# Statistics with one token a partition for three RMS norms, and another order of values, residuals, squares and weight splits at their joins

## What is computed

```python
def rmsnorm(x, g):
    xf = x.astype(jnp.float32)
    y = xf * lax.rsqrt(jnp.mean(xf * xf, axis=-1, keepdims=True) + EPS)
    return (y * g.astype(jnp.float32)).astype(x.dtype)
...
h = rmsnorm(x, norm_g[layer, 0]) * (1 + sc1) + sh1
y = mixer(h)                        # layer 0: convolution and retention; layer 1: attention
x = x + g1 * y
h = rmsnorm(x, norm_g[layer, 1]) * (1 + sc2) + sh2
x = x + g2 * (jnp.square(jax.nn.relu(h @ mlp_w1[layer])) @ mlp_w2[layer])
```

## Time and profile before

| | us |
|---|---|
| median of 3 runs | 1574.41 |
| lowest, highest | 1573.16, 1574.59 |
| the profiled execution | 1574.52 |
| its span in the profile | 1572.7 |
| TensorE busy | 1552.5 |
| VectorE busy | 985.1 |
| ScalarE busy | 625.1 |
| GpSimd busy | 486.8 |

### The profile page before, as it was taken

The page is one execution under the profiler, slowest core; times in us unless marked ns, Lnnn a source line. Parts: engine busy times, 40 slices in busy tenths (PEclk is TensorE's granted clock), DMA queues, the critical chain, the costliest instruction groups (busy, mean ns, idle before and its releaser), DMA issues.

```text
span 1572.7 us, 28646 instructions
## 1 busy us (share of the span) xinstructions
PE 1552.5 (99%) x11928; PEld 1507.6 (96%) x11928; DVE 985.1 (63%) x1820; ACT 625.1 (40%) x1149; POOL 486.8 (31%) x350
## 2 busy tenths in 40 slices
PE   8999999999999999999999999999999999999998
PEld 7999999999999999999999999889999999999998
DVE  5348677675774765555555886773585765556555
ACT  5323333344532344234334534653443334523443
POOL 0233313314223343144235243101333344324431
PEclk9999999999999999999999999999999999999999
DMA  9454333313243344344343121001221232223212
GB/s 327 156 186 143 121 119 111 101 54 117 72 161 108 122 134 135 108 146 136 112 143 134 35 81 61 28 1 54 81 81 54 68 108 68 81 67 105 70 55 81
DMA packets 133409, 162.22 MB, mean 103 GB/s; under 512 B 4640, under 2 KB 108064, under 8 KB 133280
## 3 DMA queue, kind: packets, MB, share of 16 engines
q1 hardware_dynamic: 132048, 159.34, 31.2%
q10 hardware_dynamic: 1232, 1.05, 0.2%
HBM read 156.44 MB, written 3.93 MB: 102 GB/s over the span
## 4 chain that ended last, share of the span: by engine, by line
PE 91%; DVE 5%; ACT 2%; issue 1%; POOL 0%; DVEq 0%; ACTq 0%
PE ps L654 59%; PE ps L1073 19%; PE ps L773 3%; PE ps L1261 2%; PE ps L1209 2%; DVE ps L1880 1%; PE ps L910 1%; PE ps L943 1%; DVE hL L1891 1%; PE ps L1236 1%; PE ps L859 1%; DVE ps L1870 1%; PE ps L939 1%; ACT wH L1305 1%; DVE xT L1841 0%
## 5 line engine op out<-in xcount | busy, mean ns | idle before, releaser
L1805 POOL TENSOR_TENSOR wL<-raw,wH 128x512 fp32r<-128x512 f32 x212 | 313.4, 1504 | 715.0 <-ACT wH L1305 554.6
L654 PE MATMUL ps<-fH,wH 128*128 128x320 f32 x1024 | 318.5, 311 | 0.2 <-DVE fL L2263 0.2
L654 PE MATMUL ps<-fH,wL 128*128 128x320 f32 x1024 | 316.4, 309 | 0.0
L654 PE MATMUL ps<-fL,wH 128*128 128x320 f32 x1024 | 316.3, 309 | 0.0
L1841 DVE SCALAR_TENSOR_TENSOR xT<-ps,modT,xT 128x192 f32<-128x192 f32 (+1 forms) x456 | 183.2, 434 | 192.1 <-PE ps L654 190.2
L1805 POOL TENSOR_TENSOR wL<-raw_high,wH 128x512 fp32r<-128x512 f32 x124 | 164.4, 1352 | 338.3 <-ACT wH L1317 209.6
L654 PE MATMUL ps<-hH,wH 128*128 128x320 f32 x704 | 221.1, 314 | 1.9 <-DVE hL L1891 1.1
L654 PE MATMUL ps<-hH,wL 128*128 128x320 f32 x704 | 217.5, 309 | 0.0
L654 PE MATMUL ps<-hL,wH 128*128 128x320 f32 x704 | 217.5, 309 | 0.0
L654 PEld LDWEIGHTS ps<-fH,wH 128*128 128x128 f32 x1024 | 192.3, 188 | 3.4 <-DVE xT L1841 1.2
L654 PEld LDWEIGHTS ps<-fL,wH 128*128 128x128 f32 x1024 | 192.3, 188 | 0.1
(11 more groups left out here) (257 smaller groups left out, 3052.5 us busy)
## 6 DMA issues: line engine op xcount, KB each, us to landing
ada<-in_ada_w SPq DMA_DIRECT2D x40, 1024.0 KB, 5.2
raw<-in_mlp_w SPq DMA_DIRECT2D x64, 512.0 KB, 3.7
raw_high<-in_mlp_w SPq DMA_DIRECT2D x64, 512.0 KB, 3.7
raw<-in_even_w_in SPq DMA_DIRECT2D x28, 512.0 KB, 5.9
pre_w<-in_ada_w SPq DMA_DIRECT2D x16, 512.0 KB, 9.1
raw<-in_odd_w_qkv SPq DMA_DIRECT2D x10, 512.0 KB, 3.6
raw<-in_even_w_out SPq DMA_DIRECT2D x8, 512.0 KB, 3.5
raw<-in_odd_w_o SPq DMA_DIRECT2D x6, 512.0 KB, 3.5
```

The costliest lines, as they stand in the source:

```text
L654: last = nc.tensor.matmul(ps[:, bank, 0:width], a_, b_, start=(k == 0 and p_ == 0), stop=(k == nk - 1 and p_ == 2))
L1805: last = nc.gpsimd.tensor_tensor(wL[:, at % 4, cs], raw(t)[:, j, cs], wH[:, at % 4, cs].bitcast(F32), ALU.subtract)
```

## The change

For norms 1 and 2, in both halves, the statistic is taken with one token a partition. TensorE makes three products of 128 tokens of `ssum` by one column of ones (`token_stat`; the third starts at token 192 of the half, so that it overlaps the second by 64). ScalarE's square root and VectorE's reciprocal have three columns. VectorE scales the identity by each of the three columns into a new buffer `diag`. TensorE multiplies ones by it (`token_spread`; of the third block only the last 64 columns), which puts 1/std of every token on all partitions, in the bank where it was before. VectorE's first value waits for that. In TensorE's order the first half's spread stands ahead of group 11, the second half's ahead of the fifth k step of the pair (2, 3).

In these joins VectorE has value 1 and low part 0 ahead of residual 11, each residual and pair of squares from then on comes later among the values, and the last pair of squares behind the first half's last low part. ScalarE's list gets high part 2 ahead of square 11, and the splits go one block at a time between high parts; the second block of the second tile comes behind square 15 and ahead of high parts 6 and 7. Norms 0 and 3 and the final one are left alone.

```diff
+TOKENS_AT = (0, P, HALF - P)
...
+        diag = nc.alloc_sbuf_tensor_at("diag", [P, 3, P], F32, offset=norm_buffers + 16 * HALF)
...
+            def token_stat(norm, half, count):
+
+                pe.wait_ge(sum_done, SUMS * (norm - 1) + count)
+                for j, c0 in enumerate(TOKENS_AT):
+                    last = nc.tensor.matmul(ps[:, 5 + half, j:j + 1], ssum[:, half, c0:c0 + P], ones[:, 0:1], start=True, stop=True)
+                last.then_inc(stat_full, 1)
+
+            def token_spread(norm, half):
+
+                pe.wait_ge(rstd_done, 2 * norm + half - 1)
+                for j, c0 in enumerate(TOKENS_AT):
+                    a_ = 64 if j == 2 else 0
+                    last = nc.tensor.matmul(ps[:, 5 + half, c0 + a_:c0 + P], ones[:], diag[:, j, a_:P], start=True, stop=True)
+                last.then_inc(spread_full, 1)
...
             tile_pair(T_WC, cH, cL, lambda n: pe.wait_ge(dve_free, V_WC + n - 3), nk=CC, nm=4,
-                      inside=(9, 2, lambda: stat(1, 0, SUM_AT(1, 3))))
+                      inside={(9, 2): lambda: token_stat(1, 0, SUM_AT(1, 3)), (11, 0): lambda: token_spread(1, 0)})
...
-                                  inside=(2, 0, lambda: stat(norm, 1, SUMS)), joint=((0, 1), (2, 3), (4, 5), (6, 7)))
+                                  inside={(2, 0): lambda: stat(norm, 1, SUMS)} if layer else
+                                  {(2, 0): lambda: token_stat(1, 1, SUMS), (2, 4): lambda: token_spread(1, 1)}, joint=((0, 1), (2, 3), (4, 5), (6, 7)))
...
-                            inside = (9, 2, lambda: stat(norm + 1, 0, SUM_AT(norm + 1, 3)))
+                            inside = {(9, 2): lambda: token_stat(2, 0, SUM_AT(2, 3)), (11, 0): lambda: token_spread(2, 0)}
...
-                     lambda half, k: pe.wait_ge(h_ready, 16 * 2 + 8 * half + k + 1), (2, 0, lambda: stat(2, 1, SUMS)))
+                     lambda half, k: pe.wait_ge(h_ready, 16 * 2 + 8 * half + k + 1), {(2, 0): lambda: token_stat(2, 1, SUMS), (2, 4): lambda: token_spread(2, 1)})
...
             def std(norm, half):
                 act.wait_ge(stat_full, 2 * norm + half - 1)
+                if norm < 3:
+                    nc.scalar.activation(x_rstd[:, 0:3], ps[:, 5 + half, 0:3], ACT.Sqrt, bias=eps[:],
+                                         scale=1.0 / D).then_inc(std_done, 1)
+                    return
...
                 square(norm, 10, v0, "half")
+                hi(norm, 0, (2,))
                 square(norm, 11, v0, "half")
-                hi(norm, 0, (2,))
-                split(t, start - 4)
+                split(t, start - 4, (0,))
                 hi(norm, 0, (3,))
+                split(t, None, (1,))
+                hi(norm, 0, (4,))
                 square(norm, 12, v0, "half")
-                hi(norm, 0, (4,))
                 square(norm, 13, v0, "half")
-                split(t + 1, start)
                 hi(norm, 0, (5,))
+                split(t + 1, start, (0,))
                 square(norm, 14, v0, "half")
                 square(norm, 15, v0, "half")
+                split(t + 1, None, (1,))
                 hi(norm, 0, (6, 7))
                 std(norm, 1)
...
             def reciprocal_std(norm, half):
                 dve.wait_ge(std_done, 2 * norm + half - 1)
+                if norm < 3:
+                    nc.vector.reciprocal(x_rstd[:, 0:3], x_rstd[:, 0:3]).then_inc(token_rec, 1)
+                    dve.wait_ge(token_rec, 2 * norm + half - 1)
+                    for j in range(3):
+                        last = nc.vector.tensor_scalar(diag[:, j, :], ident, x_rstd[:, j:j + 1], None, ALU.mult)
+                    last.then_inc(rstd_done, 1)
+                    return
...
             def h_value(norm, half, k):
 
+                if norm in (1, 2) and k == 0:
+                    dve.wait_ge(spread_full, 2 * norm + half - 1)
...
                 h_lo(norm, 0, KC - 1)
+                for step in later.get("last", ()):
+                    step()
                 reciprocal_std(norm, 1)
                 h_half(norm, 1)
...
-                h_both(norm, {"first": [later(8)], 0: [later(9), later(10)], 1: [later(11)],
-                              2: [squares(4), later(12)], 3: [later(13), squares(5)], 4: [later(14)],
-                              5: [later(15)], 6: [squares(6)], 7: [squares(7)]})
+                h_both(norm, {"first": [later(8)], 0: [later(9), later(10)], 2: [later(11)], 3: [squares(4), later(12)],
+                              4: [later(13)], 5: [squares(5), later(14)], 6: [later(15)], 7: [squares(6)], "last": [squares(7)]})
```

More of the change, by code:

```diff
@@ L411, in hybrid_step @@
         w_done, hh_done = sem("w_done"), sem("hh_done")
+        spread_full, token_rec = sem("spread_full"), sem("token_rec")
         h_ready, rstd_full, rstd_held = sem("h_ready"), sem("rstd_full"), sem("rstd_held")
@@ L718, in waits @@
                             w_wait(t + n // nm, k, nk)
-                        if inside and inside[:2] == (n, k):
-                            inside[2]()
+                        if inside and (n, k) in inside:
+                            inside[n, k]()
                         if x_wait and n % nm == 0:
@@ L757, in waits @@
                             w_wait(t + n // 2, k, KC)
-                        if inside[:2] == (n, k):
-                            inside[2]()
+                        if (n, k) in inside:
+                            inside[n, k]()
                         if n in (0, 4):
@@ L1147, in mlp @@
                             hooks = {1: [lambda: part(c)(2)]}
-                            inside = (9, 2, lambda: stat(norm + 1, 0, SUM_AT(norm + 1, 3)))
+                            inside = {(9, 2): lambda: token_stat(2, 0, SUM_AT(2, 3)), (11, 0): lambda: token_spread(2, 0)}
                         else:
                             hooks = {11: [first_outputs], 13: [early_outputs]}
-                            inside = (9, 2, lambda: token_sums(0))
+                            inside = {(9, 2): lambda: token_sums(0)}
                         tile_pair(t + 2, fH, fL, free, lambda half, tile, k: pe.wait_ge(f_ready, f + F_AT(c, half, k) + 1)
@@ L1286, in _ @@
             tile_pair(T_WO + 2, hH, hL, lambda n: pe.wait_ge(dve_free, V_WO + 8 + n - 3),
-                      inside=(4, 6, lambda: stat(3, 0, SUM_AT(3, 5))))
+                      inside={(4, 6): lambda: stat(3, 0, SUM_AT(3, 5))})
             mlp(1, 3)
```

## The result

The changed kernel takes 1578.72 us, median of ten runs (1577.64 to 1580.53). The kernel before took 1574.26 us on the same chip (1573.16 to 1575.42, ten runs). The ratio is 1.003, 95% interval 1.0021 to 1.0039: **4.5 us slower**, where 3.5 were forecast.

What follows compares the result with a forecast made beforehand. It took TensorE, busy 1552.5 us of a 1572.7 us span, as the bound; +2.1 us in norm 1 and +1.35 in norm 2 made +3.5, so 1577.9 from a median of 1574.41, range 1574.8 to 1579.7.

Steps and rivals of the forecast that it cites:

- Passes: TensorE in each half of norms 1 and 2: one-column products and spreads replace one sum, 0.77 us more, four halves 3.1.
- the 0.9 worked out ahead: Forecast total in us if one-column products were all but free, by the skill page's rule, instead of 3.5.
- N1a: TensorE's stretch from norm 1's first statistic to its second; forecast +0.77 us against the kernel before.
- First half, norm 1: Split holds high part 6; low part 6 ends at 422.7, so TensorE stays 0.77 us late behind its wait.
- The walk: Step-by-step timing of the engines' lists through both norms, some forty terms of half a microsecond; it gave +3.5 us.
- Second half, norm 1: Values begin 4.88 us behind the statistic instead of 3.50; third pair of groups ends at 441.3; norm 1 in all +2.1.
- N1b: TensorE's stretch from norm 1's second statistic to the first strips; forecast +1.3 us against the kernel before.
- Norm 2: Same walk, half a microsecond of added work hidden at the projection's start; values from 890.4 instead of 889.1; +1.35 us.
- A: Rival for both norms: cheap products (+0.9 us) or high part 6 not held by the split (+1.6); about 1575.7, chance 0.28.
- second branch: Of A: products as priced, but high part 6 ahead of the split, low 6 1 us earlier in both norms; +1.6 us.
- B: Rival: faster, 1569.6 or 1570.5, if low 6 ends before about 421.4 so TensorE never waits in first halves; chance 0.10.
- C: Rival: restarts and new weights between groups make products and spreads 0.8 + 0.8 a half; +4.6 to +5, 1579.2, chance 0.10.

Runs made afterwards that it cites:

- e9: The e6 kernel with one-token statistics and spreads in the first halves of norms 1 and 2; 1574.52 us, kernel before 1574.49, ratio 1.0002.
- e6: Kernel before, statistics unchanged, with a third order on VectorE and ScalarE (residuals later, high parts earlier, last split last); 1572.82 us, ratio 0.9988.
- e3: Changed kernel with high part 6 ahead of squares 14 and 15, high part 7 behind them, last split block last; 1575.78 us, ratio 1.0011.
- e8: Changed kernel with the second halves' spread issued twice into the same bank; 1579.73 us, ratio 1.0035.
- e2: Kernel before with only the new VectorE and ScalarE orders, statistics as before; 1577.07 us, ratio 1.0019.
- e5: The e2 kernel with the edit of e3 (high parts 6 and 7 and last split moved), statistics as before; 1574.39 us, ratio 1.0001.
- e1: Changed kernel with VectorE's and ScalarE's orders of before, so the one-token statistics alone; 1579.2 us, ratio 1.0033.
- e4: The e3 kernel with the full sum, square root and reciprocal of before in the second halves; 1573.28 us, ratio 0.9995.
- e7: Changed kernel with the second halves' spread two k steps earlier, ahead of the third instead of the fifth; 1578.65 us, ratio 1.003.
- e10: The e5 kernel with the query projection starting on half of its first weight block's low part; 1574.25 us, ratio 0.9999.

## Why the prediction was right

The forecast was slower, 1577.9, from a sum of +3.5; measured is +4.46, and +4.19 between the landmarks. Sign, mechanism and the four places are right. By its steps:

- **Passes.** 0.66 + 0.65 - 0.54 = 0.77 a half was forecast from the final norm's one-column products and the 128-column row. Measured: 0.67 + 0.67 - 0.54 = 0.80. The three spreads together cost six times 0.11, so the 64-column one is not seen to cost less. The Trainium skill's page "TensorE: Matmul & The Clock Gate", section "Step-by-step: what each phase is for", has throughput as N cycles alone. The trace disagrees: one column, 0.22 us a product. By that rule the sum would be the 0.9 worked out ahead, and e9's N1a would equal e6's; it is 0.80 longer.
- **First half, norm 1.** The walk had DVE's first value at 407.4 and measured is 407.64 (0.14 of that the start). Squares 6 end at 420.05 where 419.9 was forecast, the same with that 0.14. The end of the wait, forecast 0.77 late, is 0.95 late. What was missing is a term that was left out, a handoff from one engine to another. DVE is past squares 6 at 420.05, the start of its next row, and ACT's square 14 starts at 420.24, 0.19 us later; the forecast had nothing there. The rest of the chain took what was forecast; from the start of low part 6 to PE are 0.60 us in both kernels (421.38 to 421.98 before, 422.47 to 423.07 after). The split ahead of high part 6 held it for 0.95 us, as the walk said; e3, which moves high part 6 ahead of both the split and the squares, takes the wait away.
- **Second half, norm 1.** Values forecast 4.88 behind the statistic, measured 5.00; N1b +1.51 for +1.3. The spread and its landing at VectorE took 0.81 (429.13 to 429.94) where 0.70 was taken. e8 shows that this end follows the values one to one.
- **Norm 2.** +0.77 for +0.56 and +0.90 for +0.8: the same two terms. Less the 2.66 by which norm 2 begins later, squares 6 end at 881.80, the 881.8 of the forecast, and PE's wait ends at 884.82, 0.77 later than before instead of 0.56; between them lies a handoff to ACT of 0.18 (884.46 to 884.64 as read). The values begin 4.38 behind the statistic (893.39 - 889.01) where 4.28 was forecast. The forecast's 886.1 and 890.4 leave out norm 1's delay; less the 2.66, measured are 886.35 and 890.73. The forecast's half a microsecond hidden by the projection's start is there: from 878.52 to 881.56 are 3.04, less the 2.66 by which the norm begins later, 0.38 (forecast 0.25) where 0.80 of work was added.
- **Size.** The sum is low by 0.7 us of stretch, in four terms of 0.1 to 0.2, all on one side. Two kinds of crossing from engine to engine account for most of it: 0.19 and 0.18 from VectorE to ScalarE in the first halves, 0.11 and 0.10 from the spread to VectorE in the second. A walk by starts in a row on one engine does not show such a gap.
- **What I did not see.** The forecast did not price the new orders by themselves. e2 shows that they cost 2.6 us in its stretches (2.9 in the median), and e5 that the places of high part 6 and of the last split are all of it: with these two moved, the new orders take the time of the kernel before (1574.39 against 1574.42). With the one-token statistics the new orders, so moved, are better than the old ones (e3 1575.78, e1 1579.2).
- **Rivals.** A's cheap products are refuted by the rows above; its second branch, high part 6 ahead of the split, did not come about. It had +1.6, and e3 has +1.58, but that agreement is luck: e3 also moves high part 6 ahead of the squares, which the branch did not, and 0.47 of its +1.58 is the strips' wait. B's condition is met nowhere in the changed kernel, and of the other kernels only e4 and e6 come out more than a microsecond of stretch under the kernel before. C's +4.6 came close, for another reason than its own: the products measured 0.67 each and not 0.8, so new weights between two groups cost no more than in a row of their kind.

Still open: why the time is up to 3.1 us longer than the span in some runs, and why e5's median does not show the gain of its stretches.

## What to carry to other kernels

A statistic with one token a partition saves VectorE and ScalarE work and costs TensorE passes that are as dear with one column as with 128 (0.11 us each here). No run here shows it to be a gain: its passes cost their full 0.80 us in norm 1's first half (e1, e9) unless they fell into another wait (e4), and in a second half the place of the spread came on top (e7, e8). Before a chain is shortened, look at what stands ahead of its last link on the other engines: here the places of one weight split of 1 us and of one high part cost 3.0 us (e2 against e5, each less its own kernel before). Moving them only took that back; the one version whose interval lies below the kernel before is e6, which has the unchanged arithmetic and a third order on both engines.

## What was not expected of the hardware

- The same wait of 2.01 us of TensorE, at the same place and for the same block, brought the granted clock down to 0.50 in e5's profile and left it at 1.00 in e2's (matmuls 0.12 us apart from 880.07 on). Before e5's wait the engine had been busy at 1.00 throughout 870 to 876 in both. Some 16 matmuls stood 0.09 us further apart, about 1.5 us in all. The Trainium skill, "TensorE: Matmul & The Clock Gate", section "What's actually happening", says that a gate sets the clock by how busy the engine has been; that a wait can bring it down agrees with e5, and why it did not in e2 no run here shows.
- The same load of 1 MB, issued at the same place, landed after at most 5.5 us in eight profiles and after 7.1 to 7.6 in four (before, changed, e1, e3), with nothing in the edits that would tell them apart; TensorE's margin for it is some 7.1.
- The time of a run is 1.75 to 1.88 us longer than its span in all 71 runs of the kernel before whose spans were taken, and in all of e2, e4, e5, e6, e8, e9 and e10. It is 2.2 to 3.1 us longer in four of ten runs of the changed kernel, four of six of e1, two of eleven of e3 (a third has 1.97) and five of six of e7. All four kernels have one-token statistics in the second halves, but so has e8. What takes this time no profile here shows.
